# Modulation chunks one at a time behind dense chunks, by a table, in an fp32 transformer kernel on one core

## The chip, the core and the metric

The kernel runs on one core of a Trainium2 chip. PE is the matmul engine (TensorE), DVE the vector engine, ACT the scalar engine, Pool is GpSimd, and SP is the engine that issues the loads. The metric is the device time of one execution in microseconds, the median of several runs of the same program. All data are float32, and batch is 1.

## What is computed

Two blocks follow each other on 256 tokens of width 1024. The first is a hybrid mixer, cross-attention to a memory of 256 tokens and a feed-forward with a short convolution. The second has two layers, in which shifts, scales and gates of every norm come from a conditioning vector ("modulation"). It works on 256 tokens `x` and, up to the second layer's attention, on 256 context tokens as well. Cut to what matters:

```python
def adaln(cvec, w_mod, b_mod):            # 9 x 1024 columns for each layer
    m = jax.nn.silu(cvec) @ w_mod + b_mod
    return [m[:, :, i] for i in range(N_MOD)]

def ffn_half_step(x, mods, g, w_gu, w_down):
    shift, scale, gate = mods
    return x + 0.5 * gate * swiglu(rms_norm(x, g) * (1 + scale) + shift, w_gu, w_down)

def second_block(...):
    for l in range(2):
        mx, mc = adaln(c, w_mod[l], b_mod[l]), adaln(c_ctx, w_mod[l], b_mod[l])
        x = ffn_half_step(x, mx[0:3], ...)       # ctx too, with mc: feeds a1, b1
        x = x + mx[5] * mixer(modulated_norm(x, g_mix[l], mx[3], mx[4]))
        x = ffn_half_step(x, mx[6:9], ...)       # feeds a2, b2
    return rms_norm(x, g_final)
```

`w_mod` is 2 x 1024 x 9216 floats. It depends on nothing but `c` and `c_ctx`, so its product can be computed at any time before the norm that uses it.

## The kernel before

**The weight stream.** All dense weights come as 246 chunks, most of 128x2048 floats (1 MB), in the order of `plan`: `w_in_*`, `w_out`, `wk`, `wv`, `wq`, `wo`, then the feed-forwards and the mixers. A feed-forward is `up0` (11 chunks), `down0` (8 chunks of 128x1408), `up1` (11), `down1` (8). The narrow one is `ffn`, on 256 tokens. The wide ones are a1, a2 and b1, on 512 columns (tokens and context together). b2 is narrow again. Between a1 and a2 stands the token mixer with its jobs `ab_a`, `ab_u`, `ab_v`, `ab_out`; between b1 and b2 attention with `k2`, `q2`, `v2`, `wo2`.

The modulation weights come as 72 more chunks of 1 MB in the same stream. All loads stand in one list, `loads`, and SP issues them in that order. Load number `at` goes to buffer `at % 3` of `raw` and waits until the load three places ahead has been used: a dense chunk when DVE has split it (`lo_ready`), a modulation chunk when PE has multiplied with it (`mod_used`). So a modulation chunk holds its buffer until PE comes to it.

**A dense chunk.** ACT rounds it to `w_hi` (line 211) two chunks ahead, DVE makes the rest, `w_lo` (line 219). Then PE does three passes for each of 16 tiles (11 in a down chunk), `hi*hi`, `lo*hi` and `hi*lo`: lines 235 to 237, 48 matmuls (33 in a down chunk), each with 256 or 512 columns.

**A modulation chunk** takes 8 products on PE (`mods_pe`, line 1538). It reads `raw` directly in fp32, puts out 32 rows at a time in one of four strips of the array, and adds to bank 7. The trace has two records for each, so 16 for a chunk. Twelve chunks make a group, that is, one norm's shift, scale and gate. A group is finished in three steps. DVE copies the bank out (`mod_rows_out`), PE sums and turns it with two small products (`mod_turn`, line 1552), and DVE adds the bias and makes scales and gates (`mod_columns`). The next group may start only when `mod_columns` of this one is done.

**What sets the order.** Each engine's program is written out by hand in the `block` functions, and nothing is scheduled. Where PE multiplies modulation chunks is a call in that text; where they are loaded is the table `MODS_DURING`: so many, right behind the second chunk (`base + 1`) of the job named. The calls stand in runs. Ahead of each of `wv` and `wq` there are 3, behind the first attention 3, in the norm of `ffn` 3 and ahead of its `down1` 3, in the two norms behind it 4 and 5. Then come 3 in the norm behind a1, 4 ahead of `ab_out`, 5 in the norm ahead of a2 and 3 ahead of a2's `down1`. The last are 5 in the norm ahead of b1 and 4 between b1's halves. 12 are spread over the first mixer and 12 over the second attention, one by one.

**A norm** on PE is a sum over 8 tiles with a matrix of ones (lines 322 and 325) into bank 6, from squares by ACT that Pool has partly added. Then DVE makes the scale of each tile, ACT `xn_hi`, DVE `xn_lo`, and the first dense chunk's matmuls follow tile by tile.

## Time and profile before

| what | us |
|---|---|
| median of 3 runs | 2279.92 (2278.54 to 2281.42) |
| the profiled execution | 2278.47 |
| its span in the trace | 2276.7 |
| PE busy with matmuls | 2130.2 (94%) |
| DVE busy | 1003.1 (44%) |
| ACT busy | 788.5 (35%) |
| Pool busy | 221.4 (10%) |

The mean granted clock of the matmul engine was 0.975 of full speed. The queues moved 314.23 MB, 138 GB/s on average. How to read the trace: times are from the span's start. A record of a matmul is longer than the distance to the next one, since matmuls overlap in the array; the distance from start to start is what a matmul costs in a run of them. "[5.99 <-DMA raw<-in_mod]" behind a row is idle time of its engine before it and what ended it.

### The profile page before, as it was taken

The page shows a single profiled execution, that of the slowest core. Times are in us where ns is not written, and L with a number is a line of the kernel's source. Part 1 is how long each engine was busy: PE and PEld are TensorE (multiplying, and loading weights), DVE is VectorE, ACT ScalarE, POOL GpSimd, SP SyncE. Part 2 cuts the span into 40 slices and gives each one's busy share as a digit, 9 for nine tenths or more (in the row PEclk, how much of TensorE's full clock was granted, in tenths as well). Part 3 has the DMA queues.
Part 4 walks back from the last instruction along what each step waited for, and adds up shares of the span by engine and source line. Part 5 has one row for each costly group of instructions (what it writes and reads, how often), then busy time and mean ns, then how long its engine had stood idle before and what let it go on. Part 6 is the DMA issues. An engine that isn't in the chain of part 4 may idle for free.

```text
span 2276.7 us, 30879 instructions
## 1 busy us (share of the span) xinstructions
PE 2130.2 (94%) x13478; PEld 1806.4 (79%) x13479; DVE 1003.1 (44%) x1284; ACT 788.5 (35%) x965; POOL 221.4 (10%) x184
## 2 busy tenths in 40 slices
PE   6987998998899999999989999899998998989997
PEld 6974987998688888878768888777886886858997
DVE  6668544766532322353442332234232234645454
ACT  5642444544432122232232222223221223444443
POOL 1000000313101001100001101110100111001101
PEclk9999999999899999999999999999999999999999
DMA  6425554455732331341342232334224223353553
GB/s 226 147 93 219 186 226 186 150 193 195 266 122 70 107 111 66 104 175 70 130 167 81 77 130 78 119 103 181 76 100 167 78 78 109 112 222 140 167 188 108
DMA packets 53687, 314.23 MB, mean 138 GB/s; under 512 B 5936, under 2 KB 12080, under 8 KB 23728
## 3 DMA queue, kind: packets, MB, share of 16 engines
q1 hardware_dynamic: 51360, 309.50, 38.2%
q10 hardware_dynamic: 2192, 2.75, 0.4%
q8 instruction: 106, 1.74, 0.3%
q14 instruction: 29, 0.24, 0.0%
HBM read 311.18 MB, written 1.05 MB: 137 GB/s over the span
## 4 chain that ended last, share of the span: by engine, by line
PE 85%; DVE 8%; DMA 3%; ACT 2%; issue 1%; SPq 0%; POOL 0%; DVEq 0%; ACTq 0%
PE psum L235 26%; PE psum L236 26%; PE psum L237 26%; DMA raw<-in_mod 3%; DVE w_lo L219 2%; PE psum L1538 2%; PE psum L1238 1%; ACT w_hi L211 1%; PE psum L1216 1%; DVE work L386 1%; PE psum L1230 0%; PE psum L1638 0%; PE psum L325 0%; PE psum L1639 0%; DMA raw<-in_w_in_r 0%
## 5 line engine op out<-in xcount | busy, mean ns | idle before, releaser
L235 PE MATMUL psum<-xn_hi,w_hi 128*128 128x256 f32 (+1 forms) x2504 | 845.9, 338 | 25.6 <-DVE xn_lo L379 11.1
L236 PE MATMUL psum<-xn_lo,w_hi 128*128 128x256 f32 (+1 forms) x2504 | 840.3, 336 | 0.0
L237 PE MATMUL psum<-xn_hi,w_lo 128*128 128x256 f32 (+1 forms) x2504 | 839.9, 335 | 0.0
L219 DVE TENSOR_TENSOR w_lo<-raw,w_hi 128x2048 fp32r<-128x2048 f32 (+1 forms) x246 | 509.3, 2071 | 424.0 <-ACT w_hi L211 423.4
L235 PEld LDWEIGHTS psum<-xn_hi,w_hi 128*128 128x128 f32 x2504 | 482.2, 193 | 83.1 <-issue 31.0
L236 PEld LDWEIGHTS psum<-xn_lo,w_hi 128*128 128x128 f32 x2504 | 482.0, 192 | 46.5 <-issue 0.7
L237 PEld LDWEIGHTS psum<-xn_hi,w_lo 128*128 128x128 f32 x2504 | 481.5, 192 | 46.9
L211 ACT ACTIVATE w_hi<-raw 128x2048 fp32r<-128x2048 f32 (+1 forms) x246 | 421.7, 1714 | 221.0 <-PE psum L237 168.4
L235 PE MATMUL psum<-h_hi,w_hi 128*128 128x512 f32 (+1 forms) x880 | 306.7, 349 | 1.8 <-POOL h_lo L1513 1.8
L236 PE MATMUL psum<-h_lo,w_hi 128*128 128x512 f32 (+1 forms) x880 | 306.0, 348 | 0.0
L237 PE MATMUL psum<-h_hi,w_lo 128*128 128x512 f32 (+1 forms) x880 | 305.8, 348 | 0.0
L1513 POOL TENSOR_TENSOR h_lo<-work,h_hi 128x512 fp32r<-128x512 f32 (+1 forms) x110 | 154.4, 1404 | 1171.2 <-ACT h_hi L1460 1171.2
L1494 DVE TENSOR_TENSOR work<-work,psum 128x512 f32<-128x512 f32 (+1 forms) x88 | 54.7, 621 | 406.6 <-ACT work L1449 406.6
L1449 ACT ACTIVATE work<-psum 128x512 f32<-128x512 f32 (+1 forms) x88 | 47.9, 544 | 509.9 <-PE psum L237 509.9
L235 PEld LDWEIGHTS psum<-h_hi,w_hi 128*128 128x128 f32 x880 | 165.5, 188 | 27.9 <-POOL h_lo L1513 2.0
L237 PEld LDWEIGHTS psum<-h_hi,w_lo 128*128 128x128 f32 x880 | 165.5, 188 | 24.6
L236 PEld LDWEIGHTS psum<-h_lo,w_hi 128*128 128x128 f32 x880 | 165.6, 188 | 24.2
L1391 DVE SCALAR_TENSOR_TENSOR xc<-psum,mods,xc 128x256 f32<-128x256 f32 x136 | 59.9, 479 | 237.1 <-PE psum L237 236.9
L318 POOL TENSOR_TENSOR work<-work 128x256 f32<-128x256 f32 (+1 forms) x59 | 59.2, 1003 | 793.3 <-ACT work L309 757.6
L1538 PE MATMUL psum<-raw,c_pad 128*32 128x256 f32 x1152 | 86.3, 428 | 51.5 <-DMA raw<-in_mod 51.5
L309 ACT ACTIVATE work<-xc 128x512 f32<-128x512 f32 (+2 forms) x56 | 33.7, 601 | 250.8 <-DVE xc L1391 208.8
L1538 PEld LDWEIGHTS psum<-raw,c_pad 128*32 128x32 f32 x1152 | 35.0, 118 | 93.3 <-DMA raw<-in_mod 63.5
(333 smaller groups left out, 1342.9 us busy)
## 6 DMA issues: line engine op xcount, KB each, us to landing
raw<-in_mod SPq DMA_DIRECT2D x72, 1024.0 KB, 4.8
raw<-in_a_up SPq DMA_DIRECT2D x42, 1024.0 KB, 4.8
raw<-in_b_up SPq DMA_DIRECT2D x42, 1024.0 KB, 4.8
raw<-in_ffn_up SPq DMA_DIRECT2D x22, 1024.0 KB, 4.8
raw<-in_a_down SPq DMA_DIRECT2D x32, 704.0 KB, 4.1
raw<-in_b_down SPq DMA_DIRECT2D x32, 704.0 KB, 4.1
raw<-in_ffn_down SPq DMA_DIRECT2D x16, 704.0 KB, 4.3
raw<-in_wo SPq DMA_DIRECT2D x8, 1024.0 KB, 4.9
```

The lines of the kernel that those rows point to most:

```text
L211: act.activation(w_hi[:, slot, 0:size], raw[:, raw_slot(("main", g)), 0:size], ACT.Copy).then_inc(hi_ready, 1)
L219: dve.tensor_tensor(w_lo[:, slot, 0:size], raw[:, raw_slot(("main", g)), 0:size], w_hi[:, slot, 0:size].bitcast(F32), ALU.subtract).then_i ...
L235: pe.matmul(out, lh, rh, start=first, stop=False, skip_group_check=group)
L236: pe.matmul(out, lh, rl, start=False, stop=False, skip_group_check=group)
L237: return pe.matmul(out, ll, rh, start=False, stop=last, skip_group_check=group)
L309: act.activation(nrm[:, tile, 0:self.w], xc[:, tile, self.span], ACT.Square).then_inc(n_sq, 1)
L318: pool.tensor_tensor(nrm[:, 0, 0:self.w], nrm[:, 0, 0:self.w], nrm[:, k, 0:self.w], ALU.add).then_inc(n_added, 1)
L1391: mm = dve.scalar_tensor_tensor(x, got, gate[:, tile, h], x, ALU.mult, ALU.add)
L1449: act.activation(b[r, 0, 0:self.w], psum[r, s.bank, 0:self.w], ACT.Silu).then_inc(ff_gate, 1)
L1494: dve.tensor_tensor(b[r, 1, 0:self.w], b[r, 0, 0:self.w], up[up_r], ALU.mult).then_inc(evacuated, 1)
L1513: pool.tensor_tensor(lo, b[r, 1:2, 0:self.w], hi.bitcast(F32), ALU.subtract).then_inc(ff_lo, 1)
L1538: mm = pe.matmul(psum[q, 7, 0:256], c_pad[:, k, C_AT - 2 * j:C_AT - 2 * j + 32], raw[:, raw_slot(("mod", m)), k * 256:(k + 1) * 256], star ...
```

## The change

The table `MODS_DURING` becomes `MODS_BEHIND`. It names for a job and one of its chunks how many modulation chunks PE does behind it, and how many places ahead of it in the stream they stand among the loads: one place for single chunks, two for groups. The same table now drives both sides. `pe_feature_major` does what it names behind each chunk but a job's last, and behind a last chunk the calls in the block take their number from it.

What moves, in chunks: ahead of `wv` 3 become 1, ahead of `wq` 3 become none. The 3 ahead of `down1` of `ffn` are gone. In the two norms behind it 4 and 5 become 0 and 3. In a1 2 stand singly behind chunks of `up0`, 4 in `up1` and 5 in `down1`, and the norm behind keeps its 3. Ahead of `ab_out` 4 become 3, and the norm ahead of a2 has 3 for 5. In a2 6 stand singly in `up0`, and the 3 ahead of its `down1` are gone. The norm ahead of b1 has 3 for 5. In b1 5 stand singly in `up0` and 4 in `down0`, and the 4 between the halves are gone. The mixer's 12, the 3 behind the first attention, the 3 in the norm of `ffn` and the 12 of the second attention stay, with the places of their loads. There are 72 as before.

The ends of the groups move with them. The turn of the second group goes from `ffn` to a1, that of the third from a1 to the mixer, behind `ab_a`. DVE's copy of the rows stands ahead of `down0` in a1 and a2, and behind the norm in the mixer.

```diff
-MODS_DURING = dict(w_out=12, wv=3, wq=3, wo=3, ffn_up0=3, ffn_down1=3, a1_up0=9, ab_a=3, ab_out=4, a2_up0=5, a2_down1=3, b1_up0=5, b1_up1=4, wo2=12)
+MODS_BEHIND = {
+    "w_in_g": {3: (12, 2)},
+    "wk": {3: (1, 1)},
...
+    "a1_down1": {0: (1, 1), 1: (1, 1), 2: (1, 1), 3: (1, 1), 5: (1, 1), 7: (3, 2)},
...
+    "b1_down0": {c: (1, 1) for c in (0, 2, 4, 6)},
...
+def mods_behind(name, c):
+
+    return MODS_BEHIND.get(name, {}).get(c, (0, 1))[0]
...
-    mods_after = {jobs[name].base + 1: count for name, count in MODS_DURING.items()}
+    mods_after = {jobs[name].base + c + ahead: count for name, behind in MODS_BEHIND.items() for c, (count, ahead) in behind.items()}
...
                 mm.then_inc(chunk_done, 1)
+                if s.c + 1 < job.n:
+                    mods_pe(pe, mods_behind(job.name, s.c))
...
-        def branch_pe(pe, norm):
+        def branch_pe(pe, norm, turn):
             pe_feature_major(pe, jobs["ab_a"], xn_hi, xn_lo, XC, before_k=norm.ready_at_first(pe))
+            turn()
...
-            mods_pe(pe, 3)
+            mods_pe(pe, mods_behind("wk", 3))
             pe_token_major(pe, jobs["wv"], C)
             cross.ready(pe, KT - 1)
-            mods_pe(pe, 3)
             pe_feature_major(pe, jobs["wq"], xn_hi, xn_lo, X)
...
-            feed0.pe(pe, lambda: mod_turn(pe), lambda: mods_pe(pe, 3))
+            feed0.pe(pe)
             between.pe(pe)
-            mods_pe(pe, 4)
             n20.pe(pe)
-            mods_pe(pe, 5)
+            mods_pe(pe, mods_behind("ffn_down1", 7))
             feed1.pe(pe, lambda: mod_turn(pe))
...
-            feed3.pe(pe, lambda: mods_pe(pe, 4), lambda: mod_turn(pe))
+            feed3.pe(pe, late=lambda: mod_turn(pe))
```

How the instructions stand, first on PE at the end of the narrow feed-forward, through the two norms behind it. "x32" counts products of line 1538 (1565 in the changed file), 8 for a chunk. Before:

```order
L237 MATMUL psum<-h_hi,w_lo 128x256
L322 MATMUL psum<-work,ones 128x256
L325 MATMUL psum<-work,ones 128x256
L1538 MATMUL psum<-raw,c_pad 32x256 x32
L322 MATMUL psum<-work,ones 128x512
L325 MATMUL psum<-work,ones 128x512 x5
L1538 MATMUL psum<-raw,c_pad 32x256 x40
L235 MATMUL psum<-xn_hi,w_hi 128x512
```

And now:

```order
L260 MATMUL psum<-h_hi,w_lo 128x256
L347 MATMUL psum<-work,ones 128x256
L350 MATMUL psum<-work,ones 128x256
L347 MATMUL psum<-work,ones 128x512
L350 MATMUL psum<-work,ones 128x512 x5
L1565 MATMUL psum<-raw,c_pad 32x256 x24
L258 MATMUL psum<-xn_hi,w_hi 128x512
```

Nine chunks in two runs have become three in one, behind the second sum.

On PE at the narrow feed-forward's last up chunk and its down half, before:

```order
L236 MATMUL psum<-xn_lo,w_hi 128x256
L237 MATMUL psum<-xn_hi,w_lo 128x256
L1538 MATMUL psum<-raw,c_pad 32x256 x24
L235 MATMUL psum<-h_hi,w_hi 128x256
L236 MATMUL psum<-h_lo,w_hi 128x256
```

And now:

```order
L259 MATMUL psum<-xn_lo,w_hi 128x256
L260 MATMUL psum<-xn_hi,w_lo 128x256
L258 MATMUL psum<-h_hi,w_hi 128x256
L259 MATMUL psum<-h_lo,w_hi 128x256
L260 MATMUL psum<-h_hi,w_lo 128x256
```

The run of three chunks between the two is gone.

On SP, the loads from the end of a1's `up1` to the mixer, before (one row names the loads that follow each other from one array):

```order
L201 DMA raw<-in_a1_up1 128x2048 x10
L201 DMA raw<-in_a1_up1_last 128x1024
L201 DMA raw<-in_a1_down1 128x1408 x8
L201 DMA raw<-in_ab_a 128x2048 x2
L201 DMA raw<-in_mod 128x2048 x3
L201 DMA raw<-in_ab_u 128x2048 x2
```

And now:

```order
L224 DMA raw<-in_mod 128x2048
L224 DMA raw<-in_a1_up1_last 128x1024
L224 DMA raw<-in_a1_down1 128x1408 x2
L224 DMA raw<-in_mod 128x2048
L224 DMA raw<-in_a1_down1 128x1408
L224 DMA raw<-in_mod 128x2048
L224 DMA raw<-in_a1_down1 128x1408
L224 DMA raw<-in_mod 128x2048
```

Single modulation loads stand between the down half's loads, one more of each to the fourth and one behind the sixth; the three ahead of `ab_u` stay where they were.

## Rows read from the trace of the kernel before

**Rows 1.** The page, section 4: chain that ended last, share of the span by engine.
```profile
PE 85%; DVE 8%; DMA 3%; ACT 2%; issue 1%; SPq 0%; POOL 0%; DVEq 0%; ACTq 0%
```

**Rows 2.** The page, section 5: operation, count | busy us, mean ns | idle before, releaser.
```profile
L1538 PE MATMUL psum<-raw,c_pad 128*32 128x256 f32 x1152 | 86.3, 428 | 51.5 <-DMA raw<-in_mod 51.5
```

**Rows 3.** Loads into tile `raw`: microseconds from issue to landing.
```profile
DMA to landing us min/median/max: 3.4/4.8/9.6
```

**Rows 4.** Windows: length, busy us (count) of PE, PEld, DVE, ACT, POOL, granted clock, DMA, GB/s.
```profile
1460.80:1466.70 5.90, 0.01 (x2) 0.00 (x0) 1.10 (x1) 0.23 (x1) 1.92 (x1) 0.78 0.62 226
1466.80:1468.60 1.80, 1.80 (x16) 0.59 (x16) 0.00 (x0) 0.07 (x1) 0.00 (x0) 0.50 1.02 426
```

**Rows 5.** Timeline, cross-attention: start, length, engine, line, operation xcount [idle before <-releaser].
```profile
277.38 1.93 PE L1538 MATMUL psum<-raw,c_pad 128*32 128x256 f32 x32
280.96 0.39 PE L235 MATMUL psum<-w_hi,xn_hi 128*128 128x256 f32 x1
...
287.52 4.57 DVE L219 TENSOR_TENSOR w_lo<-raw,w_hi 128x2048 fp32r<-128x2048 f32 x2 [1.38 <-ACT w_hi L211]
...
304.17 1.93 PE L1538 MATMUL psum<-raw,c_pad 128*32 128x256 f32 x32
...
309.17 0.39 PE L235 MATMUL psum<-xn_hi,w_hi 128*128 128x256 f32 x1
```

**Rows 6.** Timeline, PE, narrow feed-forward: first and last down half.
```profile
456.24 0.29 PE L235 MATMUL psum<-h_hi,w_hi 128*128 128x256 f32 x1
...
488.26 0.53 PE L1552 MATMUL psum<-row_sums,mrow 128*128 128x32 f32 x4
...
553.23 0.28 PE L237 MATMUL psum<-xn_hi,w_lo 128*128 128x256 f32 x1
553.46 1.07 PE L1538 MATMUL psum<-raw,c_pad 128*32 128x256 f32 x16
...
595.54 0.59 PE L322 MATMUL psum<-work,ones 128*128 128x256 f32 x2
```

**Rows 7.** Timeline, PE, norm behind a1: its three chunks, second dense chunk's start.
```profile
986.96 1.93 PE L1538 MATMUL psum<-raw,c_pad 128*32 128x256 f32 x32
...
1006.02 0.39 PE L235 MATMUL psum<-xn_hi,w_hi 128*128 128x512 f32 x1
```

**Rows 8.** Timeline, Pool and PE, the two norms behind the narrow feed-forward.
```profile
602.43 2.80 POOL L318 TENSOR_TENSOR work<-work 128x512 f32<-128x512 f32 x2 [7.50 <-ACT work L2050]
...
607.72 2.08 PE L322 MATMUL psum<-work,ones 128*128 128x512 f32 x2
...
614.55 2.80 PE L1538 MATMUL psum<-raw,c_pad 128*32 128x256 f32 x48
...
637.33 0.39 PE L235 MATMUL psum<-xn_hi,w_hi 128*128 128x512 f32 x1
```

**Rows 9.** Timeline, PE, norm ahead of b1: its chunks, second dense chunk's start.
```profile
1534.29 1.93 PE L1538 MATMUL psum<-raw,c_pad 128*32 128x256 f32 x32
...
1557.32 0.39 PE L235 MATMUL psum<-xn_hi,w_hi 128*128 128x512 f32 x1
```

**Rows 10.** Timeline, vector engine and PE, ahead of `ab_out`.
```profile
1098.98 2.36 DVE L1707 TENSOR_TENSOR xn_lo<-work,xn_hi 128x1024 fp32r<-128x1024 f32 x2
...
1100.68 0.80 PE L235 MATMUL psum<-xn_hi,w_hi 128*128 128x512 f32 x1
```

**Rows 11.** Timeline, PE: a2's last up half to down, b1's half to half.
```profile
1458.56 0.39 PE L237 MATMUL psum<-xn_hi,w_lo 128*128 128x512 f32 x1
...
1477.48 0.39 PE L235 MATMUL psum<-h_hi,w_hi 128*128 128x512 f32 x1
...
1727.49 0.40 PE L237 MATMUL psum<-h_hi,w_lo 128*128 128x512 f32 x1
...
1753.00 0.39 PE L235 MATMUL psum<-xn_hi,w_hi 128*128 128x512 f32 x1
...
1763.88 0.39 PE L235 MATMUL psum<-xn_hi,w_hi 128*128 128x512 f32 x1
```

More of the change, by code:

```diff
@@ L70, with __init__ @@
 C_AT = 2 * MOD_GROUP - 2
-MODS_DURING = dict(w_out=12, wv=3, wq=3, wo=3, ffn_up0=3, ffn_down1=3, a1_up0=9, ab_a=3, ab_out=4, a2_up0=5, a2_down1=3, b1_up0=5, b1_up1=4, wo2=12)
+MODS_BEHIND = {
+    "w_in_g": {3: (12, 2)},
+    "wk": {3: (1, 1)},
+    "wq": {3: (3, 2)},
+    "wo": {3: (3, 2)},
+    "ffn_down1": {7: (3, 2)},
+    "a1_up0": {c: (1, 1) for c in (1, 3)},
+    "a1_up1": {c: (1, 1) for c in (2, 4, 6, 8)},
+    "a1_down1": {0: (1, 1), 1: (1, 1), 2: (1, 1), 3: (1, 1), 5: (1, 1), 7: (3, 2)},
+    "ab_v": {1: (3, 2)},
+    "ab_out": {3: (3, 2)},
+    "a2_up0": {c: (1, 1) for c in (1, 2, 4, 6, 8, 9)},
+    "a2_down1": {7: (3, 2)},
+    "b1_up0": {c: (1, 1) for c in (1, 3, 5, 7, 9)},
+    "b1_down0": {c: (1, 1) for c in (0, 2, 4, 6)},
+    "v2": {0: (12, 2)},
+}
+def mods_behind(name, c):
+    return MODS_BEHIND.get(name, {}).get(c, (0, 1))[0]
 class Job:
-    def __init__(self, base, n, size, dram, packed_last=None):
-        self.base, self.n, self.size, self.dram, self.packed_last = base, n, size, dram, packed_last
+    def __init__(self, name, base, n, size, dram, packed_last=None):
+        self.name, self.base, self.n, self.size, self.dram, self.packed_last = name, base, n, size, dram, packed_last
     def size_at(self, c):
@@ L110, in build @@
     for name, n, size, dram in plan:
-        job = jobs[name] = Job(len(sizes), n, size, dram, io.get(f"{name}_last"))
+        job = jobs[name] = Job(name, len(sizes), n, size, dram, io.get(f"{name}_last"))
         sizes += [job.size_at(c) for c in range(n)]
@@ L1463, in act, with dve @@
                     run_act(act, jobs[f"{self.name}_down{half}"], then.act_squares_after(act) if half else None)
-            def dve(self, dve, halfway=None, late=None):
+            def dve(self, dve, halfway=None, late=None, before_down=None):
                 for half in range(2):
@@ L1500, in dve @@
                         late()
+                    if not half and before_down is not None:
+                        before_down()
                     run_dve(dve, jobs[f"{self.name}_down{half}"], dve_add_gated(dve, 1, self.gate, self.w // T))
@@ L1645, in branch_pe @@
             mm.then_inc(g_pe, 1)
-            mods_pe(pe, 4)
+            mods_pe(pe, mods_behind("ab_v", 1))
             pe.wait_ge(g_dve, 12)
@@ L1674, in branch_act, with branch_dve @@
             run_act(act, jobs["ab_out"], then.act_squares_after(act))
-        def branch_dve(dve, norm):
+        def branch_dve(dve, norm, rows_out, columns):
             norm.dve(dve)
-            for name in ("ab_a", "ab_u", "ab_v"):
+            rows_out()
+            run_dve(dve, jobs["ab_a"], None)
+            columns()
+            for name in ("ab_u", "ab_v"):
                 run_dve(dve, jobs[name], None)
@@ L1880, in _ @@
             att1.pe(pe)
-            mods_pe(pe, 3)
+            mods_pe(pe, mods_behind("wq", 3))
             pe.wait_ge(at_lo, att1.heads)
@@ L1884, in _ @@
             ffn.pe(pe)
-            mods_pe(pe, 3)
-            feed0.pe(pe, lambda: mod_turn(pe), lambda: mods_pe(pe, 3))
+            mods_pe(pe, mods_behind("wo", 3))
+            feed0.pe(pe)
             between.pe(pe)
-            mods_pe(pe, 4)
             n20.pe(pe)
-            mods_pe(pe, 5)
+            mods_pe(pe, mods_behind("ffn_down1", 7))
             feed1.pe(pe, lambda: mod_turn(pe))
             n21.pe(pe)
-            mods_pe(pe, 3)
-            branch_pe(pe, n21)
+            mods_pe(pe, mods_behind("a1_down1", 7))
+            branch_pe(pe, n21, lambda: mod_turn(pe))
             n22.pe(pe)
-            mods_pe(pe, 5)
-            feed2.pe(pe, lambda: mod_turn(pe), lambda: mods_pe(pe, 3))
+            mods_pe(pe, mods_behind("ab_out", 3))
+            feed2.pe(pe, lambda: mod_turn(pe))
             n23.pe(pe)
-            mods_pe(pe, 5)
-            feed3.pe(pe, lambda: mods_pe(pe, 4), lambda: mod_turn(pe))
+            mods_pe(pe, mods_behind("a2_down1", 7))
+            feed3.pe(pe, late=lambda: mod_turn(pe))
             n24.pe(pe)
@@ L2195, in _ @@
             ffn.dve(dve)
-            mod_rows_out(dve)
-            feed0.dve(dve, lambda: mod_columns(dve))
+            feed0.dve(dve)
             between.dve(dve)
             n20.dve(dve)
-            mod_rows_out(dve)
-            feed1.dve(dve, lambda: mod_columns(dve))
-            branch_dve(dve, n21)
+            feed1.dve(dve, lambda: mod_columns(dve), before_down=lambda: mod_rows_out(dve))
+            branch_dve(dve, n21, lambda: mod_rows_out(dve), lambda: mod_columns(dve))
             n22.dve(dve)
-            mod_rows_out(dve)
-            feed2.dve(dve, lambda: mod_columns(dve))
+            feed2.dve(dve, lambda: mod_columns(dve), before_down=lambda: mod_rows_out(dve))
             n23.dve(dve)
```

## The prediction

> **What bounds the kernel now.** I first read the chain of work that ended last: 85% of it is PE [rows 1]. So an edit is worth what it does to the PE's timeline, and a wait on another engine counts only where PE waits for it. Then the costliest groups: the modulation matmuls (line 1538) are 1152 records, 16 per chunk, 72 chunks, and PE sat idle 51.5 us before them, all of it until a modulation chunk had landed [rows 2]. A load of the weight stream takes 4.8 us from issue to landing at the median, 3.4 to 9.6 in all [rows 3]. Last, PE's timeline at each place where a run of modulation chunks stands, for the distance between dense work before and behind it.
>
> Why the runs wait: three buffers hold the whole stream, and a modulation chunk gives its buffer back only when PE has used it. Three chunks can be loaded ahead of a run. The third waits for the split of a dense chunk close by, and a fourth starts only when the first is used. In the runs that stand in dense work this idling is exposed. In a norm, part lies beside vector and scalar work.
>
> A second cost stands beside the wait. After 5.9 us of idling the granted clock is 0.50 [rows 4], the lower of its two levels, 1.2 GHz, so the 16 records of a chunk fill 1.8 us, where two chunks in a row at full clock take 1.93 together [rows 5]; the dense matmuls behind it start slowly too. The Trainium skill, "TensorE: Matmul & The Clock Gate", Part 1, says that the throttled state is the default and activity releases it; by this, the trace agrees, each long wait removed gives its slow restart back as well.
>
> **What PE no longer does.** The profiled execution is 2278.5 us long (span 2276.7), 1.4 below the median of the runs shown; the sum is made against it. I take distances between the same two points, so waits and slow restarts are in them.
>
> 1. Cross-attention norm and value projection. Three chunks stand ahead of `wv` from 277.38 to 280.96, and one will: 3.6 - 1.1 = 2.5. Three stand ahead of `wq` from 304.17 to 309.17, and none will: 5.0 + 0.1 = 5.1. Together 7.6 [rows 5]. What is late next: the splits of the third and fourth chunk of `wv` end at 289.8 and 292.1, since the vector engine does the norm first. `wv` would start at 278.4; four of its chunks fill 280.96 to 304.0, so one takes 5.8, and the third is due at 290.0. It just fits, so I keep 7.6; if it doesn't, it loses 0 to 2.
> 2. Narrow feed-forward, ahead of its last down projection. From the end of the up chunks (553.23 + 0.12) to the norm (595.54) are 42.2 us. The first half has the same work without modulation: 456.24 to 488.26, 32.0 [rows 6]. It includes a short wait for the last hidden tile, which appears again here when its cover goes. Gain 10.2.
> 3. The two norms behind it. Four chunks stood in the first, five in the second. Now the second's sum over tiles can start when Pool's additions end, 602.43 + 2.80 = 605.2, not at 607.72. It took 614.55 - 607.72 = 6.8, so it ends at 612.1. From there a norm with three chunks takes 19.1 to the end of its first dense chunk (986.96 to 1006.02, the norm behind feed-forward a1, whose three chunks stay) [rows 7]. That is 631.2 against 637.33 [rows 8]: 6.1. Between 4 and 7, since the sum may restart slower.
> 4. The norms ahead of a2 and b1 go from five chunks to three. The second takes 1557.32 - 1534.29 = 23.0, against the same 19.1: 4.0 [rows 7, 9]. The first repeats the pattern, so 8.0 for two.
> 5. Token mixer: four chunks to three ahead of `ab_out`. The vector engine's last gated product is done when the rows of 1098.98 start, and PE restarts at 1100.68, so at most 1.7 is to be had and I take it; the scalar and vector work is late next [rows 10].
> 6. a2, ahead of its last down projection, three chunks go. The last up matmul starts at 1458.56, the second down chunk at 1477.48: 18.9, less 0.2, where 33 wide matmuls of 0.227 take 7.5. Gain 11.2 [rows 11].
> 7. b1, between its halves, four chunks go: 1727.49 + 0.23 to 1753.00 are 25.3 us, where a chunk takes 1763.88 - 1753.00 = 10.9 [rows 11]. Gain 14.4.
>
> Sum: 7.6 + 10.2 + 6.1 + 8.0 + 1.7 + 11.2 + 14.4 = 59.2 us.
>
> **What PE does in their place.** 26 chunks now stand alone between dense chunks: two and four in a1's up halves, five in its last down half, six in a2, five and four in b1. The trace has no single chunk between wide dense matmuls. The nearest row is the first chunk behind the narrow up half: it starts 0.23 behind a dense matmul, where narrow dense ones follow each other at 0.12 (192 of them in 23.0 us, rows 5), so 0.11 for the step in. It lasts 1.07, of which 0.16 overlaps with what follows, as a dense record lasts 0.28 at that distance [rows 6]. With another 0.11 for the step back: 0.91 + 0.22 = 1.13, and 26 x 1.13 = 29.4 us. Its ends are 0.91 (23.7 us) and 1.69 (44), the latter if each side of the step takes as long as a wide matmul's record, 0.39 [rows 11]. I take 1.13, since that row has a dense neighbour, and the higher end no row at all.
>
> The Trainium skill, "TensorEngine Tiling (Array Packing)", Tiling Modes, speaks against this part: changing the tiling mode drains TensorE, and the change makes 52 such switches where there were few. The row shows 0.11 for one. What a drain costs behind a wide matmul no run here shows; the fourth rival prices it.
>
> Everything else keeps its count. Six turns of the modulation rows remain: one leaves the narrow feed-forward and one enters the token mixer, behind `ab_a`. There the vector engine waits for the turn and then works about a microsecond while PE has the two chunks of `ab_u`, already split, so nobody waits. The copy of the rows waits for the last chunk of a group, which is used a dense chunk or more before; behind it on the vector engine stand a split and the down half's additions, none due sooner.
>
> SP's queue is the place to look for a new wait. A load behind a modulation load now waits until PE has used an earlier modulation chunk. The worst is a1's last down half, where dense and modulation loads take turns: a down chunk is asked for when a chunk is used (0.9 into the next place), lands after 4.8, and needs two splits of at most 2.3 each [rows 3, 5]: 10.3 us. It is due two down chunks later, 2 x (7.5 + 1.1) = 17.2. Even a landing of 9.6 leaves 2 us. So I cost this at nothing; its cover is those two chunks. In bandwidth it is under 2.1 MB in 8.6 us, 245 GB/s, where 426 were moved in one window [rows 4].
>
> **The forecast**: 2278.5 - 59.2 + 29.4 = 2248.7 us, 1.3% faster.
>
> **The rivals.**
> - *Norms stay where they are* (0.12). The gains 1, 3, 4 rest on vector and scalar work keeping their times when PE comes earlier. For it speaks that the vector engine's norm is in the way of the splits of `wv` by 0.2 us already. If 1, 3 and 4 give only half, 10.9 us are lost: 2260. Against it: norm a1 shows three chunks beside the same work in 19.1 us.
> - *The ring runs dry* (0.05), the rival on the other side. If a held buffer makes the next dense chunk late by more than its slack, PE waits at each single chunk. From 29.8 / 26 = 1.15 us each it eats the whole gain; a quarter of a landing exposed at each, 1.2, gives 2280, and half, 2.4, gives 2311, slower. Against it stands the slack of 2 to 7 us above.
> - *The clock falls* (0.03). If a single chunk in dense work counted as a pause, each would take 1.0 more at the low level [rows 4], and the dense matmuls behind it, by an estimate, as much again: 26 x 2.0 = 52 more, 2301, slower. The pairs of chunks behind dense work in rows 5 kept the full rate, and so did the dense matmuls after the short waits there, which speaks against.
> - *The steps cost more* (0.10): a drain of 0.39, the length of a wide matmul's record [rows 11], at each side: 26 x (0.91 + 0.78) = 44 instead of 29.4, so 2263. Rows 6 speak against it, but for a narrow neighbour only.
> - *The change doesn't do what it says* (under 0.01): the order shows the 26 places and the runs gone.
>
> **How the numbers follow.** The forecast has 0.70, with 2242 to 2256 as its own range: 0.91 instead of 1.13 gives 5.7 less, a restart or split that comes late gives up to 7 more. The first and fourth rival reach 2263. I give 2241 to 2262 as the range. A measurement of this kernel can tell 0.2%, 4.6 us, from no change. Faster by more: 0.70 + 0.12 + 0.10 less a little = 0.91. Slower by more: the ring and the clock, 0.06. Within: 0.03.
>
> **What would show it.** In the profile after: idle time of PE ahead of the modulation matmuls falls from 51.5 to some 20 us, what is left being third chunks in norms; no wait of PE for w_lo inside a1, a2, b1; each single chunk 1.13 us from dense to dense; from 553 on, the narrow down half in 32 us; the granted clock at 1.00 through b1's middle and a2's end; the norms ahead of a2 and b1 19.1 us each. Wrong would be: PE waiting for w_lo or for a modulation chunk behind single ones, a step above 0.3, or `wv` stopping at its third chunk by more than 2 us.

## The result: 2257.2 us, 1.1% faster

| | before | changed |
|---|---|---|
| median of four runs | 2280.67 us | 2257.16 us |
| lowest to highest | 2278.54 to 2285.22 | 2255.24 to 2258.81 |
| profiled execution, its span | 2278.47, 2276.7 | 2258.81, 2257.0 |
| idle of PE ahead of modulation matmuls | 51.5 us | 12.1 us |

The ratio is 0.9894, with a 95% interval of 0.9877 to 0.9911. The forecast was 2248.7, its range 2241 to 2262: the sign and the range held, and the gain came out at 23.5 us where 29.8 were forecast. The profiled execution is the highest of its four.

The page of the changed kernel, where [rows 1] and [rows 2] stood. The modulation line is now 1565, and the matmul lines are 258 to 260:

```profile
PE 87%; DVE 8%; ACT 3%; issue 1%; DMA 1%; POOL 0%; SPq 0%; DVEq 0%; ACTq 0%; POOLq 0%
...
L1565 PE MATMUL psum<-raw,c_pad 128*32 128x256 f32 x1152 | 77.5, 390 | 12.1 <-DMA raw<-in_mod 12.1
```

DMA fell from 3% to 1% of the chain. The waits of PE, by line and by what it waited for (us in total, times, longest), first of the changed kernel:

```profile
PE psum L347 <- POOL work L343: 16.9, 2, 9.1
PE psum L258 <- DVE xn_lo L404: 16.2, 5, 6.7
PE psum L1565 <- DMA raw<-in_mod: 12.1, 4, 3.4
...
PE psum L258 <- POOL h_lo L1540: 3.6, 2, 1.8
```

and of the kernel before:

```profile
PE psum L1538 <- DMA raw<-in_mod: 51.5, 20, 6.2
PE psum L235 <- DVE xn_lo L379: 11.1, 3, 6.7
PE psum L322 <- POOL work L318: 9.0, 1, 9.0
```

20 waits for a modulation chunk became 4. Some of that idling only got another name: PE now waits 7.9 us more for Pool and 5.1 more for `xn_lo`, in norms in which modulation chunks lay before. This is why the steps are read as distances between the same two points, and not as a difference of waits.

The places that answer to [rows 11] and, with the two rows at 1520.35 and 1539.53, to [rows 9], PE's timeline of the changed kernel (start, length, engine, line):

```profile
1455.84 0.39 PE L258 MATMUL psum<-h_hi,w_hi 128*128 128x512 f32 x1
...
1463.54 0.39 PE L258 MATMUL psum<-h_hi,w_hi 128*128 128x512 f32 x1
...
1520.35 1.93 PE L1565 MATMUL psum<-raw,c_pad 128*32 128x256 f32 x32
...
1539.53 0.39 PE L258 MATMUL psum<-xn_hi,w_hi 128*128 128x512 f32 x1
...
1713.17 0.50 PE L258 MATMUL psum<-h_hi,w_hi 128*128 128x512 f32 x1
...
1720.97 0.39 PE L258 MATMUL psum<-xn_hi,w_hi 128*128 128x512 f32 x1
...
1731.90 0.39 PE L258 MATMUL psum<-xn_hi,w_hi 128*128 128x512 f32 x1
```

A down chunk takes 7.70 us at a2's end, and 7.80 at b1's middle, where a single stands ahead of it; the up chunk behind it takes 10.9. There is no wait between: a2's end and b1's middle are dense through. The granted clock is 1.00 in both (windows; length, busy us of PE, PEld, DVE, ACT, POOL, clock, DMA, GB/s):

```profile
1456.00:1470.00 14.00, 14.00 (x62) 11.22 (x61) 6.93 (x6) 4.40 (x5) 1.94 (x1) 1.00 0.35 111
1721.00:1735.00 14.00, 14.00 (x63) 11.58 (x62) 6.29 (x6) 4.00 (x4) 0.77 (x1) 1.00 0.41 152
```

The norm ahead of b1 takes 19.2 us (1520.35 to 1539.53), where the forecast had 19.1.

One of the 26 single chunks, in a1's first up half:

```profile
627.12 0.39 PE L260 MATMUL psum<-xn_hi,w_lo 128*128 128x512 f32 x1
627.44 1.07 PE L1565 MATMUL psum<-raw,c_pad 128*32 128x256 f32 x16
628.44 0.50 PE L258 MATMUL psum<-xn_hi,w_hi 128*128 128x512 f32 x1
628.78 0.40 PE L259 MATMUL psum<-xn_lo,w_hi 128*128 128x512 f32 x1
```

Dense matmuls follow each other at 0.23. Here 1.32 us lie from the start of the last dense matmul ahead to that of the first behind, so 1.09 are the single's, and the next distance is 0.34. Over a whole stretch, the dense chunk with a single behind it takes 11.97 instead of 10.88 and the next one 11.05: 1.26 together. PE waits for nothing at any of the 26.

### The profile page after: what moved, and what is told of

It reads as the page before. It is cut to its first block, busy times and chain, and to the rows that moved or that the text cites. A ratio compares the mean times of both kernels' runs of the same rounds, so it can differ in the third digit from the quotient of the medians.

```text
span 2257.0 us, 30880 instructions
## 1 busy us (share of the span) xinstructions
PE 2131.1 (94%) x13479; PEld 1804.6 (80%) x13479; DVE 1004.2 (44%) x1284; ACT 788.7 (35%) x965; POOL 221.7 (10%) x184
## 4 chain that ended last, share of the span: by engine, by line
PE 87%; DVE 8%; ACT 3%; issue 1%; DMA 1%; POOL 0%; SPq 0%; DVEq 0%; ACTq 0%; POOLq 0%
PE psum L258 26%; PE psum L259 26%; PE psum L260 26%; PE psum L1565 2%; DVE w_lo L242 2%; PE psum L1263 1%; PE psum L1241 1%; ACT w_hi L234 1%; DVE work L411 1%; DMA raw<-in_mod 0%; PE psum L350 0%; PE psum L1255 0%; PE psum L1666 0%; PE psum L1667 0%; DMA raw<-in_w_in_r 0%
## 5 line engine op out<-in xcount | busy, mean ns | idle before, releaser
L258 PE MATMUL psum<-xn_hi,w_hi 128*128 128x256 f32 (+1 forms) x2504 | 847.7, 339 | 33.7 <-DVE xn_lo L404 16.2
L260 PEld LDWEIGHTS psum<-h_hi,w_lo 128*128 128x128 f32 x880 | 166.9, 190 | 24.2
L343 POOL TENSOR_TENSOR work<-work 128x256 f32<-128x256 f32 (+1 forms) x59 | 59.2, 1004 | 773.0 <-ACT work L334 736.9
L334 ACT ACTIVATE work<-xc 128x512 f32<-128x512 f32 (+2 forms) x56 | 33.6, 601 | 244.1 <-DVE xc L1416 200.9
L1565 PE MATMUL psum<-raw,c_pad 128*32 128x256 f32 x1152 | 77.5, 390 | 12.1 <-DMA raw<-in_mod 12.1
L1485 ACT ACTIVATE h_hi<-work 128x512 fp32r<-128x512 f32 (+1 forms) x110 | 60.1, 547 | 78.9 <-DVE work L1519 78.9
```

The costliest lines, as they stand in the source:

```text
L258: pe.matmul(out, lh, rh, start=first, stop=False, skip_group_check=group)
L260: return pe.matmul(out, ll, rh, start=False, stop=last, skip_group_check=group)
L343: pool.tensor_tensor(nrm[:, 0, 0:self.w], nrm[:, 0, 0:self.w], nrm[:, k, 0:self.w], ALU.add).then_inc(n_added, 1)
L1485: act.activation(out, b[r, 1:2, 0:self.w], ACT.Copy).then_inc(ff_hi, 1)
L1565: mm = pe.matmul(psum[q, 7, 0:256], c_pad[:, k, C_AT - 2 * j:C_AT - 2 * j + 32], raw[:, raw_slot(("mod", m)), k * 256:(k + 1) * 256], star ...
```

## The theories

I use "step" for what a change from dense to modulation matmuls and back costs beyond the matmuls themselves. Mine: the gain is the removed waits and slow restarts (56 to 59 us) less 26 singles at 1.23 to 1.26, and the shortfall is a dearer step between dense and modulation matmuls, plus the granted clock, which falls or doesn't fall behind the same short wait from one execution to the next. The rivals: the excess is in each chunk's body or load and not in the step; the slower places are caused by the change and would show each time.

## Experiments

**The changed kernel again.** No edit.

> The changed kernel once more, unaltered, for its profile. Theory (the clock after a short idle stretch is chance): the dense chunks of the two down halves of the narrow feed-forward, which took 3.89 us each in the first profile of the changed kernel and 3.74 us before, are free to differ from half to half again, and some half is back at 3.74; the single modulation chunks cost 1.26 us each in the wide up stages again, being code and not clock. Rival (the changed order of loads slows the narrow down halves each time): both halves are at 3.89 from their third chunk on again, and the kernel before never shows it. Time 2255 to 2259 us either way.

2256.67 us, ratio 0.9902 (0.9885 to 0.9919). The singles cost the same to 0.01 us each. In the first narrow down half the second chunk took 3.89 where the first profile had 5.40; in the second half it took 5.31, and the later chunks 3.74, where the first profile had 3.89. So these differ between executions of one kernel.

**The kernel before again.** No edit.

> The kernel before once more, unaltered, for its profile. By the theory that the clock after a short idle stretch is chance, the places that differed in unchanged code (the first down half of the narrow feed-forward, the chunk behind ab_a's norm) move here too, by some tenths of a us to 2 us each, and sometimes show 3.89 us chunks. By the rival that the change causes them, they stand as in the first profile of before (3.74 us chunks in both down halves, which end 0 to 0.3 us from where they did). Time 2278 to 2283 us.

2280.56 us. Its first narrow down half showed what the first profile of before had not: 5.41 for the second chunk and 3.89 for the others. The rival that the change causes this falls. Windows of the two first profiles over the second down chunk of that half, changed kernel and then before:

```profile
451.17:456.57 5.40, 5.40 (x35) 5.40 (x34) 2.93 (x3) 1.38 (x1) 0.00 (x0) 0.68 0.89 284
```
```profile
462.00:466.00 4.00, 4.00 (x38) 4.00 (x37) 3.01 (x3) 1.39 (x1) 0.00 (x0) 1.00 0.94 299
```

5.40 against 3.74 is the granted clock, 0.68 against 1.00. 3.89 against 3.74 is not: a window over such chunks (457 to 475) has 1.00 too. I have no cause for it.

**No singles.** The load list and the matmul loop skip the 26 chunks, so their part of the modulation is missing from this kernel's result.

```diff
+                if m in left_out:
+                    continue
...
```

> The changed kernel with the 26 modulation chunks that stand alone between dense chunks left out, loads and matmuls both; their part of the modulation is missing from the result, everything else stands. What it measures is the whole price of the 26 steps. The prediction's sum: 29.4 us (26 x 1.13), so 2257 - 29.4 = 2228 us. What the trace of the changed kernel reads chunk by chunk: 32.0 us (26 x 1.23), so 2225 us. Rival, that a single is nearly free because TensorE would otherwise wait for weights or evictions there: under 24 us, above 2233 us. Rival, that the singles also delay loads or slow chunks elsewhere: over 36 us, under 2221 us.

2224.80 us, ratio 0.9752 (0.9736 to 0.9768): 31.9 us below the changed kernel on the same chip. The four stretches with singles (a1's first up half, its second up half and down half, a2's first up half, b1's first up and down half) took 537.67 us together, exactly what they take in the kernel before, against 569.68 with singles in all three profiles of the changed kernel: 32.0. So the singles cost 1.23 each, all of it local; they delay no load and hide no wait.

**Threes in place of singles.** 24 of the 26, in the same stages:

```diff
-    "a1_up1": {c: (1, 1) for c in (2, 4, 6, 8)},
-    "a1_down1": {0: (1, 1), 1: (1, 1), 2: (1, 1), 3: (1, 1), 5: (1, 1), 7: (3, 2)},
+    "a1_up1": {2: (3, 2), 5: (3, 2), 8: (3, 2)},
+    "a1_down1": {7: (3, 2)},
-    "a2_up0": {c: (1, 1) for c in (1, 2, 4, 6, 8, 9)},
+    "a2_up0": {2: (3, 2), 6: (3, 2)},
-    "b1_up0": {c: (1, 1) for c in (1, 3, 5, 7, 9)},
-    "b1_down0": {c: (1, 1) for c in (0, 2, 4, 6)},
+    "b1_up0": {2: (3, 2), 5: (3, 2), 8: (3, 2)},
```

> The changed kernel with 24 of the 26 lone chunks put together in threes, each three behind one dense chunk of the same wide stages and two places ahead in the load order: 8 steps instead of 24. Theory: a step costs about 0.35 us over its chunks' own 0.91 us (1.26 - 0.91), for going from dense matmuls to modulation matmuls and back, so 16 steps fewer give 16 x 0.35 = 5.6 us: about 2251.5 us. Rival, that the excess is part of each chunk's own matmuls or of its load: no change, 2257 us. Rival, that three loads in a row leave the dense chunks behind them late: slower, and TensorE waits for weights (w_lo) in a1, a2 or b1.

2253.86 us, ratio 0.9881 (0.9866 to 0.9896). That is 2.8 us under the changed kernel on the same chip, and the intervals overlap, so the time alone is no proof. The timeline is: the three stretches fell by 2.06, 1.54 and 1.96, together 5.6, as expected. A three:

```profile
818.76 0.39 PE L259 MATMUL psum<-xn_hi,w_lo 128*128 128x512 f32 x1
819.08 2.80 PE L1564 MATMUL psum<-raw,c_pad 128*32 128x256 f32 x48
821.81 0.50 PE L257 MATMUL psum<-xn_hi,w_hi 128*128 128x512 f32 x1
822.15 0.40 PE L258 MATMUL psum<-xn_lo,w_hi 128*128 128x512 f32 x1
```

A chunk with a three takes 13.70, with a single 11.97: (13.70 - 11.97) / 2 = 0.865 for each chunk more. A single costs 1.26, so a step costs 0.40 over the body. The rival, all in the body, falls. No wait for `w_lo` came.

**b1's middle alone**, in the kernel before:

```diff
-MODS_DURING = dict(w_out=12, wv=3, wq=3, wo=3, ffn_up0=3, ffn_down1=3, a1_up0=9, ab_a=3, ab_out=4, a2_up0=5, a2_down1=3, b1_up0=5, b1_up1=4, wo2=12)
+MODS_DURING = dict(w_out=12, wv=3, wq=3, wo=3, ffn_up0=3, ffn_down1=3, a1_up0=9, ab_a=3, ab_out=4, a2_up0=5, a2_down1=3, b1_up0=5, wo2=12)
+SINGLE = {"b1_down0": (0, 2, 4, 6)}
...
+    mods_after.update({jobs[name].base + c + 1: 1 for name, at in SINGLE.items() for c in at})
...
+                if s.c in SINGLE.get(job.name, ()):
+                    mods_pe(pe, 1)
...
-            feed3.pe(pe, lambda: mods_pe(pe, 4), lambda: mod_turn(pe))
+            feed3.pe(pe, late=lambda: mod_turn(pe))
```

> The kernel before with one part of the change alone: the run of four modulation chunks between b1's halves goes, and the four stand one each behind chunks 0, 2, 4 and 6 of b1's first down half. Theory, by the traces of both kernels: the boundary falls by 14.3 us (the wait for the four loads, the late weights behind it and the slow restart), four singles cost 1.23 each in the down half, 4.9 us: 14.3 - 4.9 = 9.4 us faster than the kernel before, about 2271 us. Rival, that the boundary's gain came from the other parts of the change (its loads elsewhere): under 5 us faster. Rival, that the clock's chances swallow it: unclear, with the chunk table still showing 14.3 less at the boundary.

2269.28 us against 2278.73 of before on that chip: 9.45 faster, ratio 0.9961 (0.9946 to 0.9976), where 9.4 was expected. From the last down chunk's start to the second up chunk's the timeline has 18.73 us where before had 32.98: 14.25 less. The four singles took 4.7 back. One part of the change alone gives what the sum has for it.

**The two waits for `h_lo` filled.** The singles of a1's first up half move behind the last up chunk of each narrow half:

```diff
+    "ffn_up0": {10: (1, 1)},
+    "ffn_up1": {10: (1, 1)},
...
-    "a1_up0": {c: (1, 1) for c in (1, 3)},
...
+                    mods_pe(pe, mods_behind(up.name, up.n - 1))
```

> The changed kernel with the two singles of a1's first up half moved behind the last up chunk of each half of the narrow feed-forward, where TensorE stands still for 1.81 us until GpSimd's h_lo is there. Theory: a chunk (about 1 us) fits into the wait, so both singles come to nothing there and 2.5 us go from a1: 2254.2 us; and the wait left is under 1 us, so the granted clock no longer falls behind it (it fell behind the second wait in both profiles of the changed kernel, and behind the first in three of five of all profiles, at 1.5 to 2.6 us each time): all down halves at 3.74 us a chunk from the second on, and up to 4 us more, 2250 us. Rival, that switching costs as much there: 2257 us. Rival, that the clock falls all the same: the second down chunk still takes 5.4 us.

2257.64 us, ratio 0.9905 (0.9891 to 0.9920), where the changed kernel has 0.9894, 0.9902 and 0.9900 in its three measurements. The time shows no gain, and a gain of 2.5 us, 0.0011 of the time, is less than such an interval can tell. The timeline shows it: last up chunk and first down chunk took 6.92 + 4.75 = 11.67 with a single between, and 5.83 + 5.84 = 11.67 without, in both halves; a1's stretch lost its 2.5. No second down chunk was slow, though the 3.89 came in one half. (Of the six profiles before this one, three had it slow in the first half, not three of five.) The same edit stands again beside the threes, below.

**Singles inside the narrow up half**, behind its chunks 3 and 6 (`"ffn_up1": {c: (1, 1) for c in (3, 6)}` in place of `a1_up0`'s line):

> The changed kernel with the two singles of a1's first up half moved behind chunks 3 and 6 of the second up half of the narrow feed-forward, where a chunk of dense matmuls takes 5.83 to 5.95 us and a weight load lands in 4.8 us. Theory that the narrow stage is bound by the chain load, w_hi, w_lo (so that one load more makes TensorE wait there): each single costs there what it costs in a1, 1.26, and beyond it a wait of up to one load, 2.6 us at 400 GB/s: 2257 to 2262 us, with a wait for w_lo or w_hi behind the singles. Rival, that the narrow stage has room: 2257 us and no wait; then the weights' chain is no bound there either, and the rule of the change to leave that stage alone is worth nothing.

2258.50 us, ratio 0.9912 (0.9896 to 0.9929). From the half's first chunk to its down half are 66.47 us, against 64.65 in the first profile of the changed kernel: 1.82 for two, 0.91 each, less than in the wide stages, and PE waits for no weight there. The first theory falls: the narrow stage has room for singles. The change's rule to put none there was not needed; keeping it costs about 0.3 us for each chunk that could have stood there.

**Three chunks ahead of the second sum**, where PE waits for Pool:

```diff
-            n20.pe(pe)
             mods_pe(pe, mods_behind("ffn_down1", 7))
+            n20.pe(pe)
```

> The changed kernel with the three modulation chunks behind the narrow feed-forward placed ahead of TensorE's second sum matmuls, where it waits 7.9 us for GpSimd, and not behind them. Theory: the three (about 2.8 us) lie in that wait and go from the path where they stood, and since TensorE is then not idle so long the sum's matmuls run at a higher clock (8.3 us in the profile of the changed kernel against 6.8 before): 1 to 3 us faster, 2254 to 2256 us. Rival, that the end of this norm hangs on the vector engines and not on the place of the three chunks: the chunk behind a1's first starts where it did, no change, 2257 us.

2259.11 us, ratio 0.9911 (0.9896 to 0.9926), no gain; the rival holds: a1's first chunk starts 28.52 us behind the start of the last narrow down chunk, in the first profile of the changed kernel 28.51. PE's timeline, and then the same place of the changed kernel:

```profile
588.38 1.07 PE L1565 MATMUL psum<-raw,c_pad 128*32 128x256 f32 x16 [3.98 <-DMA raw<-in_mod]
590.40 2.08 PE L347 MATMUL psum<-work,ones 128*128 128x512 f32 x2 [0.95 <-POOL work L343]
...
605.27 0.77 PE L258 MATMUL psum<-xn_hi,w_hi 128*128 128x512 f32 x1 [6.49 <-DVE xn_lo L404]
```
```profile
588.88 2.07 PE L347 MATMUL psum<-work,ones 128*128 128x512 f32 x2 [7.86 <-POOL work L343]
590.74 6.53 PE L350 MATMUL psum<-work,ones 128*128 128x512 f32 x10
597.20 2.80 PE L1565 MATMUL psum<-raw,c_pad 128*32 128x256 f32 x48
603.75 0.47 PE L258 MATMUL psum<-xn_hi,w_hi 128*128 128x512 f32 x1 [3.75 <-DVE xn_lo L404]
```

The three did go into the wait for Pool, which shrank from 7.86 to 0.95. But the wait for `xn_lo` behind the sum grew from 3.75 to 6.49: the norm's end hangs on the vector engines, and wherever the three stand they are covered. The sum itself ran no faster, 8.4 us in both profiles.

**Threes and filled waits together**, with both edits from above:

> Both edits at once: the 24 lone chunks of the wide stages in threes, and the two of a1's first up half in the two waits for h_lo of the narrow feed-forward. Theory: the profiles gave 5.6 us for the threes (24 x 1.23 = 29.5 against 8 x 2.99 = 23.9) and 2.5 us for the two in the waits, whose two dense chunks took 11.67 us together with a single between them and 11.67 without: 8.1 us off the changed kernel on the same chip, about 2248.5 us, and no second down chunk of 5.4 us in either half, where 9 of the 15 waits of this kind that were left open had one. Rival, that one of the gains was chance: half of it or less, 2252.5 us or above.

2249.22 us, ratio 0.9854 (0.9839 to 0.9869). The changed kernel beside it on the same chip gave 2259.35: 10.1 us less, where 8.1 were expected, and the intervals of their ratios don't touch (0.9839 to 0.9869 against 0.9883 to 0.9916). This is the best version of the study. Its first filled wait:

```profile
448.67 1.07 PE L1566 MATMUL psum<-raw,c_pad 128*32 128x256 f32 x16
449.67 0.38 PE L258 MATMUL psum<-h_hi,w_hi 128*128 128x256 f32 x1
...
453.97 0.38 PE L258 MATMUL psum<-h_hi,w_hi 128*128 128x256 f32 x1 [0.61 <-POOL h_lo L1541]
```

against the open wait of the changed kernel:

```profile
450.72 0.38 PE L258 MATMUL psum<-h_hi,w_hi 128*128 128x256 f32 x1 [1.81 <-POOL h_lo L1540]
```

The wait is down from 1.81 to 0.61. A single chunk ahead of a wait takes its 1.2 us from the wait.

**One place of the array in place of four.** All modulation matmuls go to the same 32 columns:

```diff
-                    q = slice(32 * (k % 4), 32 * (k % 4) + 32)
-                    mm = pe.matmul(psum[q, 7, 0:256], c_pad[:, k, C_AT - 2 * j:C_AT - 2 * j + 32],
+                    mm = pe.matmul(psum[0:32, 7, 0:256], c_pad[:, k, C_AT - 2 * j:C_AT - 2 * j + 32],
...
-                                   start=(j == 0 and k < 4), stop=(j == MOD_GROUP - 1 and k >= 4), tile_position=(0, 32 * (k % 4)),
-                                   skip_group_check=True)
+                                   start=(j == 0 and k == 0), stop=(j == MOD_GROUP - 1 and k == KT - 1), skip_group_check=True)
...
-            dve.tensor_copy(mrow[:, :], psum[:, 7, 0:256]).then_inc(mod_rows, 1)
+            dve.tensor_copy(mrow[0:32, :], psum[0:32, 7, 0:256]).then_inc(mod_rows, 1)
```

> The changed kernel with every modulation matmul put into one place of 32 columns of TensorE's array, one after the other, where before four of them ran side by side at the four places. Theory of the body: four places side by side are worth a factor of four, a chunk's body goes from 0.87 us to 3.4 us, and the 26 singles alone cost 26 x 2.6 = 67 us more. Theory of the step: the 0.40 us that a step takes over the body (0.09 ahead, 0.17 behind, the rest in the filling) comes with the change from dense to modulation matmuls as such, so it stays between 0.3 and 0.5 us here. Rival, that it comes with the four places (array taken apart and put together): it goes to under 0.15 us, and the first dense matmul behind a single stands 0.23 us ahead of the second, as in the dense stretches, and not 0.34.

2393.92 us. A run of three chunks in a norm, and the same single as above:

```profile
622.22 10.55 PE L1564 MATMUL psum<-raw,c_pad 128*32 128x256 f32 x48
...
654.37 0.39 PE L260 MATMUL psum<-xn_hi,w_lo 128*128 128x512 f32 x1
654.69 3.64 PE L1564 MATMUL psum<-raw,c_pad 128*32 128x256 f32 x16
658.26 0.50 PE L258 MATMUL psum<-xn_hi,w_hi 128*128 128x512 f32 x1
658.59 0.40 PE L259 MATMUL psum<-xn_lo,w_hi 128*128 128x512 f32 x1
```

The body can be read by itself: three chunks last 10.55 and one 3.64, so (10.55 - 3.64) / 2 = 3.46 for each chunk more, four times 0.865. The two dense chunks took 14.55 + 11.01, so 3.80 for the single, and the step is 0.34. The distance into the single (0.32) and the one behind its first dense matmul (0.33) stand as they did. So most of the step doesn't come from four places side by side, which cut the body by four. The matmuls still use a 32-column place, so whether the step is the array's tiling or the change from `fp32r` to `f32` operands stays open; it wasn't tried. The Trainium skill, "TensorEngine Tiling (Array Packing)", Tiling Modes, says that a change of mode drains TensorE; that a step has a price the runs show, that this is its reason they don't.

**The changed kernel a third time**, for the direct comparison above:

> The changed kernel unaltered a third time, beside the two others on one chip, for a direct comparison and for two more of the waits for h_lo. Time 2255 to 2259 us; by the count so far (9 of 15) one of its two halves of the narrow feed-forward shows a second down chunk of 5.3 to 5.4 us.

2259.35 us, ratio 0.9900 (0.9883 to 0.9916). Neither half had a slow second chunk. Over all profiles, the second down chunk took 5.3 to 5.4 us behind 9 of 19 open waits of 1.81 us, and behind none of the 6 filled ones. If it made no difference which 9 of the 25 were slow, all six filled ones would be spared about 1 time in 22, and the two passages of one profile may not be independent. That is a hint that filling the wait keeps the clock, not a proof.

**Longer runs.** From the threes and filled waits:

```diff
-    "a1_up1": {2: (3, 2), 5: (3, 2), 8: (3, 2)},
+    "a1_up1": {5: (9, 2)},
-    "a2_up0": {2: (3, 2), 6: (3, 2)},
+    "a2_up0": {4: (6, 2)},
-    "b1_up0": {2: (3, 2), 5: (3, 2), 8: (3, 2)},
+    "b1_up0": {2: (5, 2), 6: (4, 2)},
```

> The kernel with the threes and the filled waits, with longer runs in their place: all nine of a1 behind one dense chunk, six behind one of a2, five and four behind two of b1. Theory: a run of up to three lies in the three slots of the ring when TensorE comes to it, and saves a step; from the fourth on a chunk must land while TensorE waits, each round of three some 5 to 8 us (a landing takes 3.4 to 4.8 us, and the third of three in a norm waited 3.3 to 4.0): a1 two rounds, a2 one, b1 two short ones, 5 x 3.5 = 17 us or more slower than with the threes, above 2266 us, and the wait for in_mod in front of modulation matmuls goes from 12 us to 30 or more. Rival, that loads keep up with any run of modulation chunks behind 10.88 us of dense work: four steps fewer, 1.6 us faster, 2247.6 us.

2282.41 us, ratio 1.0000 (0.9988 to 1.0012): all of the gain is gone, 33 us over the threes, where 17 or more were expected. PE waits 36.4 us for modulation chunks again, in 16 waits. In the run of nine:

```profile
851.60 2.80 PE L1566 MATMUL psum<-raw,c_pad 128*32 128x256 f32 x48
857.57 1.94 PE L1566 MATMUL psum<-raw,c_pad 128*32 128x256 f32 x16 [3.17 <-DMA raw<-in_mod]
860.05 1.93 PE L1566 MATMUL psum<-raw,c_pad 128*32 128x256 f32 x16 [0.55 <-DMA raw<-in_mod]
862.90 1.94 PE L1566 MATMUL psum<-raw,c_pad 128*32 128x256 f32 x16 [0.91 <-DMA raw<-in_mod]
```

Three chunks (48 records) are there in 2.80. The fourth waits 3.17, and from then on a chunk of 16 records takes 1.94 where it took 1.07: the granted clock is 0.50 from 857 to 868, its lower level. Each stretch with long runs lost against the profile with threes: that with the nine 15.3 us, that with the six 9.7, that with the five and four 13.7. Of these 38.6 (the profiled execution is 6 us above its median), 24 are waits of PE for modulation chunks (36.4, there 12.1). Most of the rest is the clock: the 12 chunks behind the first three of each run take 1.3 to 1.94 and not 1.07, and the dense chunk behind each run is longer by 0.6 to 2.0. My price had the waits and not the clock. So three in a row, the ring's size, is the most that came without a wait in dense work.

## Why the prediction was right, and where it was short

Each row is the distance in us between the same two chunk starts. Before: two profiles of it, and the one of b1's middle alone, which has its code (not in step 7). After: the three of the changed kernel.

| step | from, to | before | after | gain | forecast |
|---|---|---|---|---|---|
| 1 | last `wk`, second `wq` chunk | 44.8 to 44.9 | 37.1 | 7.8 | 7.6 |
| 2 | last narrow up, last down chunk | 44.3, 45.6, 45.4 | 36.5, 35.7, 34.1 | 9.7 | 10.2 |
| 3 | last narrow down, second a1 chunk | 45.5, 46.5, 44.9 | 41.2, 39.6, 40.5 | 5.2 | 6.1 |
| 4 | `ab_out` to a2 | 39.5, 39.5, 40.8 | 35.6 | 4.3 | 4.0 |
| 4 | a2 to b1 | 33.6, 33.6, 33.7 | 29.8, 30.8, 29.8 | 3.5 | 4.0 |
| 5 | last `ab_v`, second `ab_out` chunk | 62.3, 62.4, 63.9 | 61.5, 63.1, 61.5 | 0.8 | 1.7 |
| 6 | last up, second down chunk of a2 | 24.1 to 24.2 | 13.1 | 11.0 | 11.2 |
| 7 | last down, second up chunk of b1 | 33.0 | 18.7 | 14.3 | 14.4 |
| | 26 singles | | | -32.0 | -29.4 |

The time came out 8.5 us above the forecast. 2.2 of them are its base, the profiled execution of before, which lies that far below the later median. The steps gave 2.6 less than forecast, the singles cost 2.6 more, and the stretch from b1's end to b2 is 1.6 longer. Together 9.0; the 0.5 that is too much can't be resolved, since the three medians of the changed kernel alone lie 2.7 us apart.

- *The waits* were sized well: 56.6 us together against 59.2. Steps 1, 6 and 7, 33 of them, came within 0.2 each. They are those where work of the same kind without the run stood elsewhere in the trace. `wv` did not stop at its third chunk.
- *Step 2* took its 32.0 us from one passage of the first half, in which the clock had stayed up. Over all profiles with the open wait, either narrow down half takes 32.0 to 34.6. One row was read as a fixed size, where it was one draw. That the averages of step 2 come within 0.5 of the forecast is in part luck: from the first profile of before to the first of the changed kernel the gain is 7.8.
- *Step 3* held its range of 4 to 7. The restart that I feared came: the second sum now starts behind an idle stretch of 7.9 us and took 8.3 us (588.88 to 597.20), not 6.8, with a granted clock of 0.50 in its first 4.1 us; 7.0 in the second profile and 7.5 in the third.
- *Step 5*: PE now waits 3.4 us for the gated product and restarts slower (the first `ab_out` chunk takes 12.6 us, before 11.8), so about half of the 1.7 is given back, the mechanism that step 3 names and that I didn't apply here.
- *The singles* are the term that was mis-sized: 26 x 1.13 = 29.4 forecast, 32.0 measured, 1.26 for one in an up half and 1.20 in a down half. The entry was right, 0.09 against 0.11. Two parts of the sum failed. "It lasts 1.07, of which 0.16 overlaps with what follows" took the overlap from a dense record; 1.00 us lie from the single's start to the next dense matmul (627.44 to 628.44), so the overlap is 0.07. And "with another 0.11 for the step back" took an entry for an exit; behind a single the dense matmuls lose 0.17 in an up half, 0.11 of it in the first distance. Of the step's 0.40, 0.09 are the entry and the rest, about 0.30, lies at the single's end and behind it. My bound (0.39 a side) covered this. The trace of before showed the 1.00 already, at the last modulation chunk ahead of `wv` and the dense matmuls behind it, the first of which starts at 280.96 [rows 5]:

```profile
279.96 1.07 PE L1538 MATMUL psum<-raw,c_pad 128*32 128x256 f32 x16 [0.65 <-DMA raw<-in_mod]
...
281.19 0.28 PE L236 MATMUL psum<-w_lo,xn_hi 128*128 128x256 f32 x1
```

With 1.00, the entry of 0.11 and the 0.11 that the distance from 280.96 to 281.19 has over 0.12, these rows give 1.22 a chunk, 31.7 us for the 26.
- *What I costed at nothing*: the turn behind `ab_a` takes 0.36 on PE (1010.58 to 1010.94) and 0.09 at the next chunk, and the one that left the narrow stage gives 0.36 back, so the turns are neutral as forecast. Loads, splits and SP's queue cost nothing that a row shows. But the stretch from b1's end to b2 took 176.5 to 176.8 us in the three profiles, where before took 174.7 to 175.1, though nothing in it changed. Most is `k2`'s only chunk, 13.5 to 13.8 against 12.4 to 12.7, behind the same wait of 6.7 us. The kernel without singles has 175.1 there, the two with threes 175.4 and 176.1. The difference lies in how long the clock stays down: 12 or 13 of this chunk's matmuls follow each other at 0.43 us and not at 0.23 in the changed kernel, 7 or 8 in the kernel before. Why that is so with singles far ahead stays open.
- *The rivals.* The ring didn't run dry: no wait of PE for `w_lo` in a1, a2 or b1, and the run without singles shows them to be local. The clock didn't fall at singles. "Norms stay" is wrong as a whole, but 0.9 of 21.7 us went its way. "The steps cost more" was the right direction at a fifth of its size, 0.10 a chunk and not 0.56.
- *The signs.* Idle time ahead of modulation matmuls was forecast at some 20 us and is 12.1: the missing part stands as waits for Pool. The narrow down half took 34.6 (544.54 to 579.13), 33.6 and 32.0 in the three profiles, where 32 was forecast; the norms ahead of a2 and b1 took 18.9 to 20.1 us, for 19.1. A single took 1.20 to 1.26, not 1.13. "A step above 0.3" stood among the signs of being wrong: in and out together it is 0.40, so this sign came, for the singles' term alone. The clock, the missing waits for `w_lo` and `wv` came as said.

## What to carry to other kernels

Where a stream shares a ring of three buffers, put work from a second stream between the dense steps in groups of up to the ring's size: smaller groups are paid in steps (0.40 us for each group here), larger ones in waits and a low clock. A chunk ahead of a wait that is there anyway is free on the timeline, 0.00 us here. When you size how much two kinds of work overlap, take it from a place where the one follows the other, not from a record of one kind. When you size a term from one passage, look whether it starts behind an idle stretch; if so, give it the spread of such passages.

## What the hardware showed that I had not expected

- Behind the same idle stretch of 1.81 us the granted clock fell in 9 of 19 passages and cost 1.65 us, and stayed in the others. 0.61 us never cost anything in 6.
- Chunks of 33 dense matmuls of 256 columns run at 3.74 us in one passage and at 3.89 in another of the same kernel, with a granted clock of 1.00 both times.
- In the kernel with one place of the array, where modulation work fills the norms almost to their end, the first dense chunk behind a norm takes 11.0 us in a1, a2 and b1, with a granted clock of 1.00; in the changed kernel 12.3 to 13.2, with 0.82 to 0.88 in the first profile. The slow restart is worth 1.3 to 2.2 us a norm.
- Four places of 32 columns side by side cut the modulation body from 3.46 to 0.87 us a chunk, a full factor of four.
